# A two-layer hybrid decoder step: weight splits and copies moved between engines in the Conformer stage, its layer norm in token halves

## What is computed

```python
def conformer_conv(x, hist, norm_g, w_pw1, b_pw1, conv_w, conv_b, ln_g, ln_b, w_pw2):
    a, g = jnp.split(rmsnorm(x, norm_g) @ w_pw1 + b_pw1, 2, axis=-1)
    u = a * jax.nn.sigmoid(g)
    y, new_hist = causal_dwconv(u, hist, conv_w)
    y = layernorm(y + conv_b, ln_g, ln_b)
    return jax.nn.silu(y) @ w_pw2, new_hist
```

## Time and profile before

| what | value |
|---|---|
| three runs | 1465.92, 1467.84, 1468.87 us; median 1467.84 us |
| profiled execution | span 1461.8 us, first to last instruction |
| between that span and the median | 6.0 us |
| TensorE busy | 1395.3 us (95%) |
| VectorE, GpSimd, ScalarE busy | 720.4 (49%), 596.9 (41%), 479.2 (33%) |
| mean granted TensorE clock | 0.989 of full speed |

### The profile page before, as it was taken

One profiled execution on the slowest core, in us unless ns is written; L12 is line 12 of the kernel. 1 busy time (PEld: TensorE's weight loads), 2 busy tenths in 40 slices (PEclk: granted clock), 3 DMA queues, 4 the chain that ended last, 5 costly groups with the idle time before them and its releaser, 6 DMA issues.

```text
span 1461.8 us, 34670 instructions
## 1 busy us (share of the span) xinstructions
PE 1395.3 (95%) x14005; PEld 1299.8 (89%) x14005; DVE 720.4 (49%) x1256; ACT 479.2 (33%) x706; POOL 596.9 (41%) x329
## 2 busy tenths in 40 slices
PE   6998998988999999999999999988999999999998
PEld 5896767767999999999999977757999999999998
DVE  5646888874535443024442376667365430144411
ACT  4375333322333222222223321227433321222221
POOL 3322333322426554445543364422255554355441
PEclk9999999999999999999999999999999999999999
DMA  6417899979323222333312566542223323332122
GB/s 185 130 54 243 296 327 322 366 270 307 94 64 96 86 79 87 94 89 90 90 57 69 143 164 157 148 115 60 69 87 90 90 76 90 101 87 86 54 84 74
DMA packets 246246, 192.56 MB, mean 132 GB/s; under 512 B 12129, under 2 KB 205106, under 8 KB 246058
## 3 DMA queue, kind: packets, MB, share of 16 engines
q1 hardware_dynamic: 244561, 188.31, 41.9%
q10 hardware_dynamic: 1181, 1.44, 0.4%
q0 software_dynamic: 400, 1.32, 0.3%
HBM read 173.03 MB, written 6.04 MB: 122 GB/s over the span
## 4 chain that ended last, share of the span: by engine, by line
PE 74%; DVE 3%; issue 2%; ACT 1%; DMA 0%; POOL 0%; SPq 0%; ACTq 0%; DVEq 0%; POOLq 0%
PE banks L1810 64%; PE banks L2243 2%; PE banks L2076 2%; PE banks L1827 1%; PE banks L2015 1%; PE banks L1957 1%; PE banks L2192 1%; DMA u_sh<-u 0%; DVE k_grp L1300 0%; SPq L610 0%; ACTq L1106 0%; PE banks L2048 0%; PE banks L1965 0%; PE banks L2246 0%; DVE sb L1363 0%
## 5 line engine op out<-in xcount | busy, mean ns | idle before, releaser
L683 POOL TENSOR_TENSOR w_l<-w_raw,w_h 128x1024 fp32r<-128x1024 f32 (+2 forms) x195 | 439.3, 2255 | 411.9 <-ACT w_h L830 397.1
L1810 PE MATMUL banks<-xa_h,w_h 128*128 128x272 f32 x1856 | 388.1, 290 | 4.4 <-DVE tmp L1633 3.3
L1810 PE MATMUL banks<-xa_h,w_l 128*128 128x272 f32 x1856 | 385.2, 289 | 0.0
L1810 PE MATMUL banks<-xa_l,w_h 128*128 128x272 f32 x1856 | 383.6, 288 | 0.0
L1810 PEld LDWEIGHTS banks<-xa_h,w_h 128*128 128x128 f32 x1856 | 292.9, 189 | 6.7 <-issue 5.5
L1810 PEld LDWEIGHTS banks<-xa_l,w_h 128*128 128x128 f32 x1856 | 292.3, 189 | 0.0
L1810 PEld LDWEIGHTS banks<-xa_h,w_l 128*128 128x128 f32 x1856 | 290.4, 189 | 0.0
L830 ACT ACTIVATE w_h<-w_raw 128x1024 fp32r<-128x1024 f32 (+2 forms) x193 | 185.1, 961 | 200.2 <-PE banks L1810 199.9
L1810 PE MATMUL banks<-h_h,w_h 128*128 128x272 f32 x928 | 193.1, 289 | 0.3 <-DVE x L1572 0.3
L1810 PE MATMUL banks<-h_h,w_l 128*128 128x272 f32 x928 | 192.6, 289 | 0.0
L1810 PE MATMUL banks<-h_l,w_h 128*128 128x272 f32 x928 | 191.9, 288 | 0.0
(11 more groups left out here) (302 smaller groups left out, 1650.8 us busy)
## 6 DMA issues: line engine op xcount, KB each, us to landing
w_raw<-in_w_up SPq DMA_DIRECT2D x88, 512.0 KB, 3.7
k_grp<-in_cache_k SPq DMA_DIRECT2D x128, 256.0 KB, 4.4
v_pg<-in_cache_v SPq DMA_DIRECT2D x120, 256.0 KB, 5.1
w_raw<-in_w_in SPq DMA_DIRECT2D x24, 512.0 KB, 6.4
w_raw<-in_w_down SPq DMA_DIRECT2D x32, 384.0 KB, 3.1
w_raw<-in_w_pw SPq DMA_DIRECT2D x24, 512.0 KB, 3.7
w_raw<-in_w_down SPq DMA_DIRECT2D x32, 320.0 KB, 3.0
w_raw<-in_w_out SPq DMA_DIRECT2D x8, 512.0 KB, 5.6
```

The costliest lines, as they stand in the source:

```text
L683: g.tensor_tensor(w_l[:, slot, 0:n], w_raw[:, slot, 0:n], w_h[:, slot, 0:n].bitcast(F32), ALU.subtract).then_inc(s_lo, 1)
L1810: ins = mm(out[:, half, 0:HT], w, v[:, half * HT:(half + 1) * HT], start=first and t == 0 and n == 0, stop=last and t == phase.tiles - 1 a ...
```

## The change

- In pw1 the low parts of the weights are subtracted by VectorE (`weights_low`, two per chunk): 13 slabs of pw1 and the first 3 of pw2, 16 in all. They count on a semaphore of their own; `low_done` says for a slab which to wait for. SyncE's loads in these phases wait for them.
- The 16 copies of a chunk are issued by SyncE (8) and GpSimd (8). For chunks 0 and 7 SyncE issues 3 and GpSimd 6, ScalarE makes four by an activation copy and VectorE three by a tensor copy.
- The pivot is the mean over chunks 0 to 4. Its sum is taken after the first slab of pw1's last turn. About this pivot only chunks 5, 6 and 7 are left in the channel sum.
- Everything from the pivot subtraction to h_l goes by halves of 272 tokens, all chunks of half 0 and then of half 1. Chunk 7's convolution is done for the left half in eight steps, then for the right half in three pieces with the sums of half 0 and a spread in between.
- The sums are laid with tokens on partitions (128x128 stationary, one column moving). VectorE forms offset and 1/sqrt on 3 columns, by a start value from the bits and three Newton steps (`inverse_root`), and TensorE spreads each over the partitions by a matmul with a broadcast column. Ln and Exp are gone from this place.
- pw2's first four slabs run side by side in eight PSUM banks, half 0 of all tiles and then half 1, with the sums of half 1 ahead of tile 2 and its spreads ahead of tile 5. The conv_c rows are turned after slab 4.

The diff, cut to its core:

```diff
+        def low_done(phase, i, j):
+            at_first = isinstance(i, int) and i == 0
+            if phase is ph["pw1"] and not (at_first and j < 3):
+                return s_lov, i * 4 + (j - 2)
+            if phase is ph["pw2"] and at_first and j < 3:
+                return s_lov, 14 + j
+            return s_lo, phase.slab(i, j) + (1 - 16 * (phase.slab0 >= ph["pw2"].slab0))
...
-                    sp.wait_ge(s_lo, s - (SLOTS - 1))
+                    if phase in (ph["pw1"], ph["pw2"]):
+                        before = order[order.index(phase) - 1]
+                        sp.wait_ge(*(low_done(phase, i - 1, j) if i else low_done(before, before.turns - 1, j)))
+                    else:
+                        sp.wait_ge(s_lo, s - (SLOTS - 1) - 16 * (phase.slab0 >= ph["pw2"].slab0))
...
-                for r, q in [(r, q) for r in range(4) for q in range(4)][:6 if c in (0, DC - 1) else 16]:
+                for r, q in [(r, q) for r in range(2) for q in range(4)][slice(3, 6) if c in (0, DC - 1) else slice(8)]:
...
+            def shifted_also(c, b):
+                edge = isinstance(c, int) and c in (0, DC - 1)
+                pool.wait_ge(s_u, c * 2 + 2)
+                if isinstance(c, int) and c == 0:
                     pool.wait_ge(s_cz, 4)
-                else:
+                if not (isinstance(c, int) and c < 2):
                     pool.wait_ge(s_cvp, c - 1)
-                for q in range(4):
-                    g.dma_start(u_sh[b][96:P, q, 3:TE], u[32 * q:32 * q + 32, c, 0:TE - 3]).then_inc(s_ush3, 16)
+                for r, q in [(r, q) for r in (3, 2) for q in range(4)] if not edge else [(3, q) for q in range(4)] + [(1, 2), (1, 3)]:
+                    g.dma_start(u_sh[b][32 * r:32 * r + 32, q, r:TE],
+                                u[32 * q:32 * q + 32, ds(c, 1), 0:TE - r].rearrange("p a t -> p (a t)")).then_inc(s_ushp[b], 16)
...
                 for j in range(4):
...
                     if j % 2:
                         tap_weights(i * 2 + j // 2, j // 2)
-                        if isinstance(i, int) and i == 0 and j == 1:
-                            shifted_also(0)
+                        shifted_also(i * 2 + j // 2, j // 2)
             turns(pool, ph["pw1"], turn, 1)
-            def turn(i, last):
-                for j in range(4):
-                    ahead(split_low, ph["pw2"], i, j, last)
-            turns(pool, ph["pw2"], turn)
+            ahead(split_low, ph["pw2"], 0, 0, False)
+            total = half_of(sq_sum, 1)
+            for m in range(1, DC - 1):
+                pool.wait_ge(s_lnq, DC + m + 1)
+                if m > 1:
+                    pool.wait_ge(s_sqq, m)
+                g.tensor_tensor(total, square(1, 0) if m == 1 else total, square(1, m), ALU.add)\
+                 .then_inc(s_sqq, 2 if m == 1 else 1)
+            for j in range(1, 4):
+                ahead(split_low, ph["pw2"], 0, j, False)
+            for j in range(4):
...
-                for r, q in [(2, q) for q in range(4)] + [(1, 2), (1, 3)]:
-                        nc.scalar.dma_start(u_sh[b][32 * r:32 * r + 32, q, r:TE], u[32 * q:32 * q + 32, c, 0:TE - r])\
-                          .then_inc(s_ush[b], 16)
+                for q in range(4):
+                    A(u_sh[b][64:96, q, 2:TE], u[32 * q:32 * q + 32, c, 0:TE - 2], ACT.Copy).then_inc(s_ushc, 1)
...
+            split_high(ph["pw2"].slab0 // 4, 3, DC)
+            def squared(half, m):
+                act.wait_ge(s_xc, 8 * half + m + 1)
+                A(square(half, m), half_of(yc[:, m, :], half), ACT.Square).then_inc(s_lnq, 1)
+            for m in range(DC - 1):
+                squared(0, m)
+            def last_squared(half):
+                act.wait_ge(s_xc, (DC, 2 * DC + 1)[half])
+                act.wait_ge((s_sqp, s_sqq)[half], 2)
+                A(square(half, 0), half_of(last_c, half), ACT.Square).then_inc(s_lnq, 1)
+            last_squared(0)
+            for m in range(DC - 1):
+                squared(1, m)
+            for e in range(2 * DC):
+                half, m = divmod(e, DC)
+                if e == 2:
+                    last_squared(1)
+                if e == 6:
+                    act.wait_ge(s_spr, 4)
+                    for to, at in zip((off_of[1], inv_of[1]), spread_at[1]):
+                        A(to, banks[:, at, 0:HT], ACT.Copy).then_inc(s_bsp, 1)
+                act.wait_ge(s_ty, e + 1)
+                if e >= 2:
+                    act.wait_ge(s_hlo, HB["pw2"] + e - 1)
+                if e == 5:
+                    act.wait_ge(s_cvl, 2)
+                A(half_of(tmp[:, m % 2, :], half), half_of(yc[:, m, :], half), ACT.Silu, scale=par("ln_g", m),
+                  bias=par("ln_b", m)).then_inc(s_s32, 1)
+                act.wait_ge(s_s32, e + 1)
+                A(half_of(h_h[:, m, :], half), half_of(tmp[:, m % 2, :], half), ACT.Copy).then_inc(s_hhi, 1)
+            for m in range(4):
+                if m < 3:
+                    split_high(ph["pw2"].slab0 // 4 + 1, m, DC)
+                norm_work("pw2", m, m % 2)
             for q in range(2):
                 rows_of(512, UT, R["conv_c"] + q, u_row[:, q * 512:q * 512 + 512])
-            residual(ph["pw2"], "pw2")
+            for j in range(4):
+                ahead(split_high, ph["pw2"], 1, j, True)
+                norm_work("pw2", 4 + j, j % 2)
...
+            def weights_low(i, j):
+                p, turn, slot = ph["pw1"], i + (j + 3) // 4, (j + 3) % 4
+                dve.wait_ge(s_hi, turn * 4 + (p.slab0 + slot + 1))
+                V.tensor_tensor(w_l[:, slot, :], w_raw[:, slot, :], w_h[:, slot, :].bitcast(F32), ALU.subtract)\
+                 .then_inc(s_lov, 1)
+            def pivot_taken():
+                dve.wait_ge(s_piv, 1)
+                V.tensor_scalar(halves(pivot[:, :]), psum_s[:, :, 64:64 + HT], 1.0 / (LN_PIVOT * P), None, ALU.mult)\
+                 .then_inc(s_pivd, 1)
+                dve.wait_ge(s_pivd, 1)
...
+                weights_low(i, 3 - 2 * b)
+                if waiting:
+                    waiting()
...
+                weights_low(i, 2 * b)
+                if first:
+                    first()
...
+                if known and c in (0, DC - 1):
+                    for q in range(3):
+                        V.tensor_copy(u_sh[b][0:32, q, 0:TE], u[32 * q:32 * q + 32, c, 0:TE]).then_inc(s_ushc, 1)
+                if known and c == 0:
+                    weights_low(i, 1)
+                else:
+                    combine(c - 1, 1 - b, i, waiting)
...
+            def first_three():
+                for m in range(3):
+                    about_pivot(0, m)
+            chunk(ph["pw1"].turns - 1, 0, True, pivot_taken)
+            chunk(ph["pw1"].turns - 1, 1, False, None, first_three)
+            for m in range(3, DC - 1):
+                about_pivot(0, m)
+            for m in range(1, DC - 1):
...
+                squares_added(m)
...
+            def last_about_pivot(half):
+                bias = par("conv_cb", DC - 1)
+                dve.wait_ge(s_cvl, half + 1)
+                parts = ((7, 0, 0, HT),) if half == 0 else ((6, HT, HT, TP), (6, 0, TP, T))
+                for at, p0, t0, t1 in parts:
+                    V.scalar_tensor_tensor(last_c[:, t0:t1], banks[:, at, p0:p0 + t1 - t0], bias, pivot[:, t0:t1],
+                                           ALU.add, ALU.subtract).then_inc(s_xc, 1)
...
+            def inverse_root(half):
+                off, sq_off, neg, y, t = (ln[:, half, k, :] for k in range(5))
+                def stepped():
+                    st.tick()
+                    after()
+                dve.wait_ge(s_lns, 2 * half + 1)
+                V.tensor_scalar(off, sums_at(half, 0, 0, 3), 1.0 / D, None, ALU.mult).then_inc(s_off, 1)
+                dve.wait_ge(s_off, half + 1)
+                V.scalar_tensor_tensor(sq_off, off, 0.5, off, ALU.mult, ALU.mult).then_inc(s_dve, 1)
+                stepped()
+                V.tensor_scalar(sq_off, sq_off, -0.5 * EPS, None, ALU.add).then_inc(s_dve, 1)
+                stepped()
+                dve.wait_ge(s_lns, 2 * half + 2)
+                V.scalar_tensor_tensor(neg, sums_at(half, 1, 0, 3), -0.5 / D, sq_off, ALU.mult, ALU.add).then_inc(s_dve, 1)
+                stepped()
+                V.tensor_scalar(y.bitcast(I32), neg.bitcast(I32), -0.5, float(0x5f3759df - (1 << 22) - (1 << 30)),
+                                ALU.mult, ALU.add).then_inc(s_dve, 1)
+                stepped()
+                for step in range(3):
+                    V.tensor_tensor(t, y, y, ALU.mult).then_inc(s_dve, 1)
+                    stepped()
+                    V.tensor_tensor(t, t, neg, ALU.mult).then_inc(s_dve, 1)
+                    stepped()
+                    if step < 2:
+                        V.scalar_tensor_tensor(y, t, 1.5, y, ALU.add, ALU.mult).then_inc(s_dve, 1)
+                        stepped()
+                    else:
```

(101 more changed lines are left out.)

250 lines of the change are left out of this document (101 added, 149 removed).

## The result

The changed kernel takes 1483.63 us (median of 6 runs, 1476.01 to 1486.72), the kernel before 1466.44 (6 runs, 1458.80 to 1468.87). The ratio is 1.0100, 95% interval 1.0079 to 1.0121: slower by about 15 us (the medians lie 17.2 apart). The forecast was +5, 1472.8 us, in a range up to 1478.0: it had the sign, and the measured time lies above the range. The profiled execution has a span of 1485.0 us and a mean clock of 0.980 of full speed; with a time of 1486.72 it is the slowest of the six. Its counterpart of before had 1461.8 us and 0.989.

A forecast was written before the change was run, and what follows sets the result against it. TensorE, busy for 95% of the span, was taken to bound the kernel with its gaps. The terms -3.1 + 0.1 + 9.05 - 0.85 gave +5.2, rounded down to +5.0: 1472.8 us, range 1465.5 to 1478.0.

The forecast's parts named there:

- Chunk 0, -3.1: Chunk 0's convolution in pw1: its 3.11 us wait for copies goes entirely, 3.1 us gained (bounds 0 to -3.1).
- Steady loop, 0: The pw1 loop: VectorE's added low parts and the split copies cost nothing, 0 us (bounds 0 to +1).
- (d): Rival: VectorE bounds the pw1 loop, its low parts twice as long; +1 us in six or seven chunks, 1479; chance 0.04.
- (e): Rival: VectorE holds up GpSimd's queue of copies in the loop; 2 us in each of six chunks, 1485; chance 0.03.
- (2): Before conv 7: three SyncE copies follow a pw2 weight load, so it starts as before, 975.2 (bounds 971.7 to 977).
- Rival (b): Faster: chunk 7's nine copies land at once, conv 7 starts at 971.7, clock stays up; 1464.9 us; chance 0.15.
- (3): Left half of chunk 7's convolution: 3.3 us and 1.8 lost to the low clock, done at 980.4.
- (4): Half 0's sum waits for VectorE's seven half 1 subtractions and an add; thought decisive; TensorE goes on at 984.9.
- (5): Half 0's twelve one-column sum matmuls: 2.9 us, plus 0.5 for an even chance of the low clock; until 988.3.
- (6): TensorE's remaining work before pw2: six right-half steps (0.4 each), samples (0.8), two spreads (1.4); until 992.9.
- Feed, 2.4: Ahead of pw2: scale, Silu of a half, copy and VectorE's other halves take 2.4 us until h_l.
- Inside pw2, +8.2: Dense pw2 stretch: 9.05 us added by half 1's sums, spreads, conv_c rows and stalls, less 0.85 for the low clock.

The follow-up runs named there:

- e9: Changed kernel with VectorE's pivot subtractions of half 1 and the sum of chunks 5 and 6 put ahead of the wait for chunk 7's left convolution; ratio 1.0044.
- e13: Changed kernel with copies first, extra matmuls, wide and gap sums, later slab order, and VectorE's half 1 work split around the left convolution's end; ratio 1.0040.
- e6: Kernel before the change with matmuls that belong to nothing (10 and 24) in TensorE's two gaps; ratio 1.0001.
- e3: Changed kernel with chunk 7's three SyncE copies put ahead of the weight load of pw2's slab 6; ratio 1.0114.
- e5: Changed kernel with matmuls that belong to nothing (26, 14 and 8) filling TensorE's gaps; ratio 1.0054.
- e2: Changed kernel with the pw1 side undone: GpSimd subtracts all low parts, copies issued as before, layer norm still in halves; ratio 1.0118.
- e1: Kernel before with only the pw1 side of the change: low parts on VectorE and the copies split; layer norm as before; ratio 1.0012.
- e7: Changed kernel with three quarters of half 1's sums moved from ahead of pw2's tile 2 into the gap before pw2; ratio 1.0110.
- e4: Changed kernel with the add of chunks 5 and 6 split by halves, half 0 added before chunk 7's pivot subtraction; ratio 1.0069.

## Why the prediction was right and wrong

**Direction: right**, and in pw2 by its own reason: half 1's sums lie in the dense stretch. The other reason, that the chain up to pw2 is no shorter than before, holds for the kernel as built. Without the wait for the sum it is shorter: 17.5 us from conv 7's start to pw2 in e9, 20.0 before.

**The base: the 6.0 us between span and median were not a fixed part.** 1.7 to 1.8 of them lie between any run's time and its span. The rest was a profiled execution faster than the median. The sum of differences does not depend on it.

**Chunk 0, -3.1: right in its place, wrong in its worth.** The wait fell from 3.11 to 0.67 us, but 2.14 came up at chunk 1, for which I had found "2 us spare even there". I had TensorE arrive at u + 12.8 and the copies at u + 11. It arrived at u + 11.2, because u came 1.6 us late behind the operation of 3.11 us. The copies landed at u + 13.3: the eight issues took 6.5 us, and the last copy landed 4.4 us after them, where I had 5 to 6 and 3. The earlier trace rows had shown a VectorE operation stretched beside GpSimd's work. I took that as gone with the splits and left out the tap expansion, which stays. Where the clock also fell in the loop (after, e13) nothing is left. In the other twelve profiled executions with the pw1 side the loop takes 129.7 to 131.1 us, against 133.1 before, 1.7 of it half clock; where that did not fall it takes 131.4 (e6).

**Steady loop, 0: right.** No other wait for copies, and none of VectorE's lateness reached TensorE, though its 2.65 us of idle time before sg are used up. Rivals (d) and (e) fall. GpSimd's eight issues took 3.95 us, 0.49 each, beside VectorE's work, as the earlier trace rows had it (0.53). At chunk 7 six issues beside VectorE's own three copies took 3.04. **The Trainium skill** ("SBUF — State Buffer", section "SBUF: two separate sides") has a 0.62 us DMA grow to 3.1 beside a two-port VectorE operation. By this trace nothing of it is seen in these issues; in which mode VectorE's operations ran it does not show.

**(2) Copies of chunk 7 at u + 8.55: mis-sized, they landed at u + 11.1** (upper bound 10.35). The order was right: behind the load. The load was issued at u + 3.7 against the forecast's 3.25 (VectorE's three copies took 1.73 us, not 1.3), and the three copies by u + 6.3. They took 4.8 us more to land, with the next load's packets behind them; I had charged 0.45 us of engine time per copy. Rival (b), copies that land at once, needed u + 5.4. e3 puts them ahead of the load and comes to u + 7.5.

**(3) and (4): close.** The left half took 5.95 us instead of 5.2, 4.5 of them at half clock. The step that "decides" did: TensorE waited 4.69 us, and from the convolution's end to the sums it was 5.4 us against my 4.5.

**(5), the step that failed, and (6) with it: what the wait of (4) does to the clock.** I gave the sums 2.9 and "0.5 for an even chance of the low clock after a gap of 3 us". The gap was 4.7, and everything up to 1003 ran at half clock: the sums 5.2 us, the right half, samples and spreads 7.2 instead of 4.6. (2) to (6) miss by 2.55 + 0.75 + 0.9 + 1.8 + 2.6 = 8.6 us, all but 0.1 of the middle's error (37.4 measured, 28.65 forecast). e9 and e5 show the cause from both sides. Without the wait the stretch from conv 7 to pw2 loses 8.7 us, and with extra matmuls in the gaps, which keep the clock up for the most part, the middle loses 4.3.

**Newton's eleven steps, 2.6 and hidden: right.** They took 2.1 us (998.43 to 1000.56), one per 0.197, and the second spread did not wait for them.

**Feed, 2.4: right** (2.46). **Inside pw2, +8.2: right, +9.3 measured.** Sums 2.9 (1011.05 to 1013.9), wait at tile 5 1.60, slab 4 1.42, each as forecast; spreads 1.4, rows 1.04. The wait at tile 4 did not come. The clock came instead: two stretches of 3.4 us at 1.2 GHz, worth 2.5 us by e2 and e5, where I had subtracted 0.85:

```profile
1022.81 0.39 PE L2452 MATMUL banks<-h_h,w_h 128*128 128x272 f32 x1 [1.60 <-DVE h_l L1893]
1042.55 0.52 PE L1944 MATMUL banks<-h_h,w_h 128*128 128x272 f32 x2 [1.42 <-POOL w_l L710]
```

**The sum.** Forecast -3.1 + 0.1 + 8.2 = +5.2. Measured by the profiles, from the mark to the sum behind pw2: -0.1 + 7.9 + 9.3 = +17.1; by the timed runs +15. By the profiles 11.9 us are missing: 8.7 in the middle, 1.1 in pw2, and 2.1 in the loop, where chunk 0's 3.1 less the pivot's 0.9 should have been gained. A range whose upper end gave the low clock 2.3 us in all was too narrow, with four new waits on the list; in the timed runs it held back 6 to 7 us more than before.

**Open.** e1, e3, e6 and e7 gain 3 to 7 us in the stage by their profiles, against the kernel that each was made from, and nothing in their medians. The clocks of the timed runs say part of it. For e3 and e7 the low clock held back as much as in the changed kernel (26.4, 26.9, 25.7), though their profiles had 3 and 5 us less half clock in the stage: in the clock these profiles were not typical. For e6 it held back less and the rest grew. For e1 nothing but the clock differs from before (20.3 against 18.1 in the same set). Why the clock did not follow the profiles stays open: each is one execution, and half clock ahead of the stage ranges from 5.1 to 22.2 us over identical code.

## What to carry to other kernels

A wait of TensorE is to be priced at its length and again at what it may do to the clock behind it: here removing 4.7 us of waiting took out 8 to 9. The second price is not fixed: in the kernel before, keeping the clock up brought nothing. Before a norm is cut in halves, list what the second half puts into a stretch that was dense (6 us here, and 2.5 of clock), since the first half's gain has to pay for it. An order tuned on one engine holds only while the other side's arrival stays where it was: moving work ahead of a wait took 10 us off the middle, and 5 of them were back once the wait ended sooner. A profile is one execution: set its clock beside those of the timed runs before crediting a few microseconds of it.

## What the runs showed of the hardware

- Executions of identical instructions reached the stage between 832.1 and 845.9 us, with 5.1 to 22.2 us held back by the clock (10 to 44 us at 1.2 GHz) ahead of it. One profile says little about a few microseconds, unless it is read from a mark inside it.
- A VectorE operation that meets a GpSimd tensor operation was stretched up to 0.3 us past the other's end: 0.47 us to 3.11 and 2.50 (128x492 and 128x491 float32, one input), 0.16 to 0.53 and 0.67 on three columns (e4). In the kernel before it went both ways: GpSimd's low part from 2.40 to 3.84 us, VectorE's multiply from 0.75 to 2.16.
- A row of 128x128 float32 matmuls with one column takes 0.11 us a pass at 2.4 GHz, 0.21 at 1.2; dependent VectorE operations on three columns follow each other every 0.197 us.
- After a wait of 4.7 us TensorE's clock stayed at half for ten microseconds in which it was busy for 9.93 (993 to 1003, granted 0.50). With matmuls without use in this gap and the others it was granted 0.83 over the same window (e5).
- In the kernel before, such matmuls raised the granted clock of the timed runs (0.990 against 0.986) and left the time as it was (1.0001).
